# Values from tokens not yet normed, and a last norm taken tile by tile beside the last product

## The reference, cut to what matters

```
xn  = rmsnorm(h, norm1_w)                      # x * rsqrt(mean(x*x) + 1e-6) * w, over 1024 features
q, k, v, g, f_lr, z, xbc, dt_raw = split(xn @ w_in)
gk  = log_sigmoid(f_lr @ w_gk2 + b_gk2) / 16
h   = h + mixers(q, k, v, g, gk, z, xbc, dt_raw) @ w_out
xn  = rmsnorm(h, norm2_w)
h   = h + peer(xn)                             # 128x128 product-key experts, gelu between two tables u and v
y   = rmsnorm(h, final_norm_w)
```

## Time and profile before

| | us |
|---|---|
| median of 3 runs | 2099.81 |
| lowest and highest run | 2093.13, 2103.64 |
| the profiled execution's own time | 2102.89 |
| its span | 2101.1 |
| TensorE matmul busy | 2022.0 |
| VectorE, ScalarE, Pool busy | 1214.1, 628.1, 1146.0 |

### The profile page before, as it was taken

The page is one execution under the profiler, slowest core; times in us unless marked ns, Lnnn a source line. Parts: engine busy times, 40 slices in busy tenths (PEclk is TensorE's granted clock), DMA queues, the critical chain, the costliest instruction groups (busy, mean ns, idle before and its releaser), DMA issues. The chain is left out here.

```text
span 2101.1 us, 31725 instructions
## 1 busy us (share of the span) xinstructions
PE 2022.0 (96%) x12559; PEld 1841.7 (88%) x12559; DVE 1214.1 (58%) x2223; ACT 628.1 (30%) x987; POOL 1146.0 (55%) x705
## 2 busy tenths in 40 slices
PE   5999999888999999999999999998999999999996
PEld 3578777776999999999999999997999999999995
DVE  2325264746699777778343331114677777777773
ACT  2224112412242323232323233223333333333331
POOL 0023320221448788888888888875466666666200
PEclk8999998989999999999999999999999999999998
DMA  3098112022235565665565555777999999999961
GB/s 147 2 340 269 41 31 86 1 89 84 71 118 124 125 126 125 123 128 126 128 130 119 126 126 123 168 187 249 313 318 323 315 322 321 320 320 320 324 201 47
DMA packets 232812, 365.34 MB, mean 174 GB/s; under 512 B 92129, under 2 KB 157170, under 8 KB 232050
## 3 DMA queue, kind: packets, MB, share of 16 engines
q1 hardware_dynamic: 154354, 294.43, 42.5%
q0 software_dynamic: 78336, 69.25, 16.8%
HBM read 290.21 MB, written 73.38 MB: 173 GB/s over the span
## 5 line engine op out<-in xcount | busy, mean ns | idle before, releaser
L833 PE MATMUL bank<-xh,usp 128*128 128x288 f32 x4320 | 754.7, 296 | 1.1 <-DVE xl L1473 1.1
L1707 POOL DMA_INDIRECT gates_scratch<-gate_val,gate_at x384 | 669.3, 1743 | 133.8 <-issue 115.8
L928 PE MATMUL bank<-W,vsp 128*128 128x448 f32 x3072 | 637.6, 369 | 9.0 <-DVE W L1602 9.0
L833 PEld LDWEIGHTS bank<-xh,usp 128*128 128x128 f32 x4320 | 636.6, 189 | 2.9 <-DVE xl L1473 1.6
L928 PEld LDWEIGHTS bank<-W,vsp 128*128 128x128 f32 x3072 | 578.8, 188 | 67.6 <-issue 9.2
L833 PE MATMUL bank<-xl,usp 128*128 128x288 f32 x2160 | 462.3, 296 | 0.0
L833 PEld LDWEIGHTS bank<-xl,usp 128*128 128x128 f32 x2160 | 348.1, 189 | 0.0
L1485 DVE TENSOR_TENSOR usp<-ring,usp 128x1024 fp32r<-128x1024 f32 x120 | 146.6, 1222 | 335.2 <-ACT usp L1096 334.8
L1597 DVE TENSOR_TENSOR vsp<-ring,vsp 128x1024 fp32r<-128x1024 f32 x128 | 156.9, 1226 | 178.1 <-ACT vsp L1181 177.6
L1729 POOL DMA_INDIRECT picked<-in_v,row_index x128 | 150.1, 1173 | 195.5 <-DVE acc L1616 167.9
L1122 ACT ACTIVATE gl<-bank 128x288 f32<-128x288 f32 x256 | 91.2, 409 | 522.1 <-PE bank L833 521.9
(11 more groups left out here) (251 smaller groups left out, 1649.6 us busy)
## 6 DMA issues: line engine op xcount, KB each, us to landing
ring<-in_u SPq DMA_DIRECT2D x128, 512.0 KB, 4.1
ring<-in_v SPq DMA_DIRECT2D x128, 512.0 KB, 5.4
hidden_scratch<-gl SPq DMA_DIRECT2D x128, 288.0 KB, 2.2
xn<-hidden_scratch SPq DMA_DIRECT2D x128, 224.0 KB, 5.7
G<-gates_scratch SPq DMA_DIRECT2D x120, 224.0 KB, 4.7
gates_scratch<-zero SPq DMA_DIRECT2D x32, 768.0 KB, 8.9
ring<-in_wproj SPq DMA_DIRECT2D x36, 512.0 KB, 3.6
gates_scratch<-gate_val,gate_at POOLq DMA_INDIRECT x384
```

What stands on the lines that cost most here:

```text
L833: mm = pe.matmul(bank[b + y][:, 0:PHALF], w, src[:, k, y * PHALF:(y + 1) * PHALF], start=(k == 0 and w is hi and src is xh), stop=(k == KT ...
L928: mm = pe.matmul(bank[(k + 4) % 8][:, 0:TA], w, W[:, n % 4, z, :], start=(n == 0 and w is hi and z == 0), stop=(n == NE - 1 and w is lo))
L1707: pool.indirect_dma_start(gates_flat, bass.IndirectOffsetOnAxis(ap=gate_at[0:r, i, x:x + 1], axis=0), gate_val[0:r, i, hh, x - hh * TOPK:x ...
```

## The change

The first norm and the values. The block of ones and epsilon are no longer loaded: VectorE writes them with memset. `prm` is loaded first, `cst` after the inputs and the small tables. VectorE writes `mix = h * norm1_w` as tiles land. The small product and the values read `mix`, not `xn`. The root is multiplied in afterwards: for `fl` by VectorE on the way out of PSUM, for the values as a scale per token in ScalarE's copies. For that, five matmuls with one row and one column turn the root into token rows (`rtok`). Value tile 0 is computed ahead of these, tiles 1 to 4 after the gate; they go to banks 2, 3, 0, 1, 2. `xn` is still made, for the projections, which wait for it tile by tile.

The last norm. In the last block each output tile counts `block_done` by itself, so that VectorE adds it while TensorE goes on. The turning of `acc` goes ahead of tile 5 of the last block. ScalarE loads Sqrt's table early, squares the 464 leading columns of each tile as it is added, and the gathered 128 columns of all tiles in one instruction, into `squares`, which lies over the buffers of the gathered rows. Pool adds the squares of tiles 2 and 3, VectorE those of 4 and 5 and of 6 and 7; TensorE sums tiles 0 and 1 singly and the three pairs.

Some semaphores that were used once are merged into counts (`fl_step`, `e_step`, `khat_step`, `hsm_keys_loaded`, `dt_step`). The diff, cut to its core:

```diff
@@ SP
+            sp.dma_start(prm[:, :], d["param"]).then_inc(prm_loaded, 16)
             for k in range(KT):
                 sp.dma_start(h[:, k, :], d["xT"][:, k, :]).then_inc(x_loaded[k], 16)
+            sp.dma_start(small[:, :, :], d["wsmall"]).then_inc(small_loaded, 16)
+            sp.dma_start(row[:, :], d["rows"]).then_inc(small_loaded, 16)
+            sp.dma_start(wgk[:, :], d["w_gk2"]).then_inc(small_loaded, 16)
             sp.dma_start(cst[:, :], d["const"]).then_inc(const_loaded, 16)
-            sp.dma_start(prm[:, :], d["param"]).then_inc(const_loaded, 16)
-            sp.dma_start(row[:, :], d["rows"]).then_inc(small_loaded, 16)
-            sp.dma_start(small[:, :, :], d["wsmall"]).then_inc(small_loaded, 16)
-            sp.dma_start(wgk[:, :], d["w_gk2"]).then_inc(small_loaded, 16)
@@ TensorE, start
-            pe.wait_ge(const_loaded, 32)
+            pe.wait_ge(ones_ready, 1)
...
-                        pe.wait_ge(normed, norm_base[0] + k + 1)
-                    mm = pe.matmul(bank[x][0:DT_ROW + SH, 0:HALF], small[:, k, :], xn[:, k, x * HALF:(x + 1) * HALF],
+                        pe.wait_ge(raw_ready, k + 1)
+                    mm = pe.matmul(bank[x][0:DT_ROW + SH, 0:HALF], small[:, k, :], mix[:, k, x * HALF:(x + 1) * HALF],
...
+            def values(i, b):
+                for k in range(KT):
+                    mm = pe.matmul(bank[b][0:rows(i), :], mix[:, k, cols(i)], wv_sb[:, k, :], start=(k == 0), stop=(k == KT - 1))
+                mm.then_inc(v_done, 1)
+
+            pe.wait_ge(wv_loaded, 16)
+            values(0, 2)
+            pe.wait_ge(fl_step, 3)
+            for i in range(TILES):
+                mm = pe.matmul(bank[4][0:rows(i), i:i + 1], sq[0:1, 0, cols(i)], ones[0:1, 0:1], start=True, stop=True)
+            mm.then_inc(rtok_ready, 1)
+            pe.wait_ge(const_loaded, 16)
...
+            values(1, 3)
+            values(2, 0)
+            values(3, 1)
+            pe.wait_ge(v_copied, 1)
+            values(4, 2)
@@ TensorE, end
+            def turn_gathered():
+                pe.wait_ge(acc_ready, 1)
+                pe.wait_ge(dense_added, 4)
+                for k in range(KT):
+                    mm = pe.transpose(bank[6 + k // 4][:, k % 4 * P:(k % 4 + 1) * P], acc[:, 0, k * P:(k + 1) * P], ident)
+                    if k % 4 == 3:
+                        mm.then_inc(turned_b, 1)
...
+                    if n == NE - 1 and k == 5:
+                        turn_gathered()
...
-                mm.then_inc(block_done, 1)
+                    if n == NE - 1 or k == KT - 1:
+                        mm.then_inc(block_done, 1)
...
-            for k in range(KT):
-                norm_sum(3, k)
+            for k, (ready, count) in {0: (sq_ready, norm_base[3] + 6), 1: (sq_ready, norm_base[3] + 6), 2: (pool_paired, 1),
+                                      4: (dve_paired, 1), 6: (dve_paired, 2)}.items():
+                pe.wait_ge(ready, count)
+                for y in range(2):
+                    mm = pe.matmul(bank[4 + y][:, 0:HALF], ones, squares[:, k, y * HALF:(y + 1) * HALF],
+                                   start=(k == 0), stop=(k == 6))
+                    if k == 6:
+                        mm.then_inc(sq_used, 1)
@@ ScalarE
+            act.wait_ge(rtok_ready, 2)
             for i in range(TILES):
                 act.wait_ge(v_done, i + 1)
-                act.activation(V[0:rows(i), i, :], bank[2 + i % 2][0:rows(i), :], ACT.Copy).then_inc(v_copied, 1)
+                act.activation(V[0:rows(i), i, :], bank[[2, 3, 0, 1, 2][i]][0:rows(i), :], ACT.Copy,
+                               scale=rtok[0:rows(i), i:i + 1]).then_inc(v_copied, 1)
...
-            norm(3, lambda k: act.wait_ge(peer_added, k // 4 + 1))
+            dense, own = slice(0, META + TA), slice(META + TA, T)
+            act.activation(gstat[:, 0, 0:1], gstat[:, 1, 0:1], ACT.Sqrt)
+            for k in range(KT):
+                if k == 5:
+                    act.wait_ge(peer_added, 2)
+                    act.activation(squares[:, :, own], h[:, :, own], ACT.Square).then_inc(sq_ready, 1)
+                act.wait_ge(dense_added, k + 1)
+                act.activation(squares[:, k, dense], h[:, k, dense], ACT.Square).then_inc(sq_ready, 1)
+            for y in range(2):
+                act.wait_ge(sq_used, norm_base[3] + y + 1)
+                act.activation(sq[:, 0, y * HALF:(y + 1) * HALF], bank[4 + y][:, 0:HALF], ACT.Sqrt,
+                               scale=1.0 / D, bias=eps).then_inc(root_ready, 1)
@@ VectorE, start
+            dve.memset(eps, EPS)
+            dve.memset(ones, 1.0).then_inc(ones_ready, 1)
...
+            dve.wait_ge(prm_loaded, 16)
+            for k in range(KT):
+                dve.wait_ge(x_loaded[k], 16)
+                dve.tensor_scalar(mix[:, k, :], h[:, k, :], pp("norm1")[:, k:k + 1], None, ALU.mult).then_inc(raw_ready, 1)
+            root(0)
+            dve.wait_ge(fl_step, 1)
+            for x in range(2):
+                half = slice(x * HALF, (x + 1) * HALF)
+                dve.tensor_tensor(fl[:, half], bank[x][0:DT_ROW + SH, 0:HALF], sq[0:DT_ROW + SH, 0, half], ALU.mult).then_inc(fl_step, 1)
             norm(0)
+            dve.wait_ge(rtok_ready, 1)
+            dve.tensor_copy(rtok[:, 0:TILES - 1], bank[4][:, 0:TILES - 1])
+            dve.tensor_copy(rtok[0:rows(TILES - 1), TILES - 1:TILES], bank[4][0:rows(TILES - 1), TILES - 1:TILES]).then_inc(rtok_ready, 1)
@@ VectorE and Pool, end
-            dve.wait_ge(block_done, NE)
-            for k in range(KT):
+            def add_dense(k):
+                dve.wait_ge(block_done, NE + k)
...
+            for k in range(5):
+                add_dense(k)
             for y in range(2):
                 dve.wait_ge(turned_b, y + 1)
...
+            for k in range(5, KT):
+                add_dense(k)
+            for k in (4, 6):
+                dve.wait_ge(sq_ready, norm_base[3] + k + 3)
+                dve.tensor_tensor(squares[:, k, :], squares[:, k, :], squares[:, k + 1, :], ALU.add).then_inc(dve_paired, 1)
...
+            pool.wait_ge(sq_ready, norm_base[3] + 6)
+            pool.tensor_tensor(squares[:, 2, :], squares[:, 2, :], squares[:, 3, :], ALU.add).then_inc(pool_paired, 1)
```

More of the change, by code:

```diff
@@ L101, in seg_cols @@
     return (0, META) if r == 0 else (META + SLEN * (r - 1), META + SLEN * r)
-CONST_PARTS = [("ident", P), ("ones", P), ("incl_a", P), ("incl_b", P), ("suf_a", P), ("suf_b", P),
+CONST_PARTS = [("ident", P), ("incl_a", P), ("incl_b", P), ("suf_a", P), ("suf_b", P),
                ("tincl_a", P), ("tsuf_a", P), ("neg_a", P), ("neg_b", P), ("col_a", P // C), ("col_b", SEGS),
-               ("head2", 2), ("iota", NK), ("iota16", TOPK), ("eps", 1), ("column", TILES)]
+               ("head2", 2), ("iota", NK), ("iota16", TOPK), ("column", TILES)]
 def offsets(parts):
@@ L130, in constants @@
     parts = {
-        "ident": np.eye(P), "ones": np.ones((P, P)),
+        "ident": np.eye(P),
         "incl_a": le & same_a, "incl_b": le & same_b, "suf_a": gt & same_a, "suf_b": gt & same_b,
@@ L171, in build @@
         cst = sb(base, "cst", [P, CONST_N])
+        ones_sb = sb(base, "ones_sb", [P, P])
+        eps_sb = sb(base, "eps_sb", [P, 1])
+        rtok = sb(base, "rtok", [P, TILES])
         zero = sb(base, "zero", [P, 1, TS // 2])
@@ L183, in pp @@
             return prm[:, a:b]
-        ident, ones = cc("ident"), cc("ones")
+        ident, ones, eps = cc("ident"), ones_sb[:, :], eps_sb[:, :]
         bank = [base.enter_context(nc.psum_tensor(f"bank{n}", [P, 512], F32)) for n in range(8)]
@@ L291, in build @@
         G = sb(ex, "G", [P, 8, TA])
+        squares = picked[:, :, :].rearrange("p a b -> p (a b)")[:, 0:KT * T].rearrange("p (k t) -> p k t", k=KT)
         vsp = sb(ex, "vsp", [P, 4, 2, D], F32R)
@@ L587, in _ @@
                 pe.matmul(out, ones[0:1, 0:rows(i)], row[0:1, :], start=False, stop=True).then_inc(gk_done, 1)
-            pe.wait_ge(wv_loaded, 16)
-            for i in range(TILES):
-                if i >= 2:
-                    pe.wait_ge(v_copied, i - 1)
-                for k in range(KT):
-                    mm = pe.matmul(bank[2 + i % 2][0:rows(i), :], xn[:, k, cols(i)], wv_sb[:, k, :],
-                                   start=(k == 0), stop=(k == KT - 1))
-                mm.then_inc(v_done, 1)
+            values(1, 3)
[3 more added lines that the diff above has]
+            values(4, 2)
             pe.wait_ge(gk_ready, 1)
-            pe.wait_ge(dtl_copied, 1)
+            pe.wait_ge(fl_step, 5)
+            pe.wait_ge(rtok_ready, 2)
             for p in range(NP):
@@ L604, in _ @@
             mm.then_inc(b_done, 1)
+            pe.wait_ge(v_copied, 4)
             for i in range(TILES):
@@ L613, in _ @@
             for n in range(4):
-                project(n, xn)
+                project(n, xn, norm=0)
             pe.wait_ge(b_copied, 4)
@@ L964, in norm @@
```

(19 more changed lines are left out.)

88 lines of the change are left out of this document (40 added, 48 removed).

## The result

The changed kernel takes 2064.12 us, the median of four runs (2062.61, 2063.39, 2064.85, 2076.30), against 2096.47 us for the kernel before, the median of four (2092.65 to 2103.64): a ratio of 0.9849 with a 95% interval of 0.9814 to 0.9883. The profiled execution took 2063.39 us, its span 2061.6, which is 39.5 less than the span before.

A forecast was written before the change was run, and what follows sets the result against it. The prediction took TensorE, busy 96% of 2101.1 us, to bound the kernel. Gains of 14.5 us at the start and 10.5 at the end, 25.0 together, gave 2074.8 from the median; forecast 2075.5, range 2066 to 2086.

The forecast's parts named there:

- Before, three runs spread over 10 us (2093 to 2104), which adds some 4 us on either side: Whole kernel: the spread of three earlier runs widens the range by some 4 us on either side.
- so it moves as a block: Everything after the values, later weight loads and zeroing writes included, starts sooner together with no further gain.
- In between: The stages between the changed start and the changed end: they move as a block, 0 us gained there.
- The end: Last norm: partly overlapped with the last product, reciprocals start 6.5 us behind its old end instead of 17.1; 10.5 us gained.
- Pool against VectorE: Sums of the last norm: Pool's add may hold VectorE's pairs, to 3.8 and 4.5 us, at no cost in direct order.
- The start: First norm to values: earlier squares, no 5.71 us wait, values end at 71.6 instead of 86.1; 14.5 us gained.
- Half clock at the start: Rival, start: a second stretch like the 8.5 us at clock 0.50 costs half of that, 2080 us; chance 0.10.
- its mirror: Rival, start: the clock stays up through the gk pause, 4 us better, 2071.5 us; chance 0.10.
- Gain given back: Rival: the start's gain is lost to a wait tied to a load, leaving the end's 10.5 us, 2089; chance 0.05.
- slower: Rival: TensorE stays at 1.2 GHz up to the end of the values, 45 us more, 2120 us; chance 0.02.

The follow-up runs named there:

- e7: Changed kernel with the turning of the gathered sum behind the whole last product instead of inside it; 2082.99 us, one run.
- e8: Changed kernel without Pool's pair, tiles 2 and 3 summed one by one; 2070.43 us, one run.
- e5: Changed kernel with value tile 1 moved ahead of the third gate product, into TensorE's 2.2 us pause; ratio 0.9855 to the kernel before, median 2064.4 us.
- e2: Changed kernel with ones, epsilon and token roots in one tile, so later tiles lie where the kernel before has them; ratio 0.9863 to the kernel before.
- e3: Changed kernel with the last norm of the kernel before, so only the start is changed; ratio 0.9906 to the kernel before, median 2083.1 us.
- e10: Changed kernel in which TensorE waits before blocks 32, 64 and 96 of the second product until its last block is done; ratio 0.9857 to the kernel before.
- e6: e5 with value tile 4 also moved behind the suffix sums, to fill the pause before the projections; ratio 0.9804 to the kernel before, median 2056.8 us.
- e1: Kernel before with 32 unused bytes a partition behind the constants, so later tiles lie as in the changed kernel; ratio 0.9986 to the kernel before.
- e4: Kernel before with the last norm of the changed kernel, so only the end is changed; ratio 0.9941 to the kernel before.
- e9: e6 with the small products spread one by one behind the matmuls of value tiles 1 and 2; ratio 0.9861 to the kernel before, median 2069.9 us.

## Why the prediction was right, and where it was wrong

The direction and the two mechanisms were right. What failed is the step "Before, three runs spread over 10 us (2093 to 2104), which adds some 4 us on either side", with the step "so it moves as a block", which put what lies between the two stages at 0. Between the two profiles it was 17.4 us, 12.5 of them in the second product. I read the spread as noise around one centre. It is in the main a draw between two times 11 to 12 us apart, to which a second one of some 7 to 9 us comes from the clock (*In between*, below). The profile that I summed from was of the slow kind (637.6 us of second product); of the three runs shown, 2103.64 lies in the slow group, 2093.13 in the quick one, and 2099.81 can't be told. A median of four that falls into the lower group, as the changed kernel's did (three of four), moves by more than the 4 us I allowed. How far outside the range it landed (1.9 us) is in part chance: another draw of four could have fallen inside it or further out. The trace of before could have told me the pace of its own execution, but not that there is another.

Point by point:

- *The end*, 10.5 forecast, 10.2 measured: reciprocals 6.9 us behind the product's own end, where I had 6.5. Tile by tile adds, turning inside the product, early table, clock at full for the sums (20 records in 5.25 us): as written. e7 shows what the turning's place is worth (8.7 against 6.9), e8 that Pool is hidden and worth 1.0.
- *Pool against VectorE*: the row that I weighed and the Trainium skill's rule (SBUF — State Buffer, Who interferes with whom) hold here: one of VectorE's pairs took 0.8 us more beside Pool (the two 2.34 us, against 0.78 each without). It cost nothing, as forecast.
- *The start*, 14.5 forecast, 11.9 between the two profiles. First Square 5.58 for 5.3. The sums took 11.2 us, not 10.0 (half pace lasted longer), the small product 8.2 for 8.0, tile 0 7.1 for 6.9, the step from dt to tile 1 10.4 as carried over, tiles 1 to 4 30.6 for 29.2 (half clock until nearly 50 us). By the averages of three profiles with the old start (93.6, 96.3, 94.7) and six with the changed one (81.7, 81.7, 81.4, 80.1, 80.7, 80.7) it is 13.8.
- *Half clock at the start*, a rival at 0.10 with its mirror: neither; a stretch of about the same length came with the pause again, but where the clock had fallen 0.7 us into the pause in before (at 43.0), in after it fell 0.3 us before the pause began, and in e5 without one. I had named the cause too simply.
- *In between*, 0 forecast. From the first projection to the product with u the old start took 436.1, 441.8 and 433.0 us in three profiles, the changed one 432.0, 432.0, 432.0, 439.0, 438.7 and 439.2 (after, e2, e3, e7, e8, e10). Windows of this stretch in after and e8 show what differs: the same records, but a lower granted clock, with TensorE busy for 6.3 of the 6.6 us more.

```profile
81.70:513.80 432.10, 406.01 (x2409) 327.10 (x2409) 221.04 (x354) 113.35 (x209) 94.30 (x38) 0.95 0.36 115
80.70:519.40 438.70, 412.27 (x2408) 331.74 (x2408) 221.30 (x354) 113.34 (x209) 94.27 (x38) 0.93 0.35 113
```

  Summed over windows of 1 us, the clock was at half for 44.4 us of the stretch in the three profiles of 432.0, for 47.8 and 51.2 in those of 433.0 and 436.1, and for 61.4 or 61.5 in the four from 438.7 to 441.8. As the ranges of the two starts overlap, the 4 us between the two profiles can't be put down to the change. Nor are they shown to be chance alone: by mean clock most runs of the changed kernel and e2 had the short stretch (nine of ten at 0.981 or 0.982, like their profiles; e7, e8 and e10 had 0.977 or 0.978), while 37 of the 42 runs of the kernel before whose clock is on record lie at 0.975 to 0.977 (its profile, with 436.1, at 0.977).
- *Gain given back* and *slower*: no sign of either.

With 13.8 and 10.2 the two stages that were changed are worth about 24 us, against 25.0 forecast. All 46 runs of the kernel before average 2097.9, and the ten runs of the changed instruction stream (with e2, which only places tiles otherwise) 2069.3; these 28.6 us carry an uncertainty of some 5 from the draws, so they don't tell 24 from a few more. The halves alone, 19.7 us (0.9906) and 12.4 (0.9941), carry some 6 each.

Left open: what in the beginning of the second product's stream decides its pace, and why the clock stays at half for 44 us of the stretch before the product with u in some executions and for 61 in others.

## What to carry to other kernels

A norm's root can be multiplied in behind the product that it would hold up, and a last norm can run beside the product whose tiles it reads; both gains came out within a microsecond or so of sums made from single rows (13.8 on average for 14.5, though 11.9 between the two profiles; 10.2 for 10.5). Before a range is set, ask of every long stage whether another execution could run it at another pace: a few times in two groups are not noise around one time. And filling a pause of TensorE with useful work need not gain the pause: 2.2 us filled brought the running sums 4.5 us forward in e5, but with 3.0 us more filled in e6 the projections started at the same 77.2, as the clock fell a second time. Look at the windows after each such step.

## What the runs showed of the hardware

- A stream of 448-column matmuls, gapless and at clock 1.00, ran at 203.5 or at 207.5 ns a record (625.3 and 637.6 us for 3072), and went from the slow to the quick pace within one execution, in the 20 us that hold a drain of TensorE (e10, once). The product with u showed one pace: 894.6 us from its first record to its last in before, and within 0.1 of that in e1 to e4 and in after.
- The granted clock fell to 0.50 while TensorE was busy for 2.00 of 2.00 us with tiny products (e5), in the middle of gate tiles between value matmuls (e9), and 0.3 us before a pause began (after); in these three no pause went before the fall.
- The same 2408 records or so between the first projection and the product with u took 432 us in one execution and 439 in another, with the clock at half for 44.4 us of it in the one (after) and for 61.4 in the other (e8).
